# Hybrid decoder trunk on one core: nine groups of eight TensorE transposes become 144 VectorE block transposes

## The reference, cut to what matters

```python
for l in range(DEPTH):                       # 2
    h = _rmsnorm(x, ln_g[l])
    u = h @ w_in[l]                          # 2048 x 6232
    (g_a, g_b, g_c, g_d, a_q, a_k, a_v, a_lr, b_xbc, b_dt,
     c_q, c_kv, c_kr, d_q, d_k, d_v) = _split(u, IN_WIDTHS)
    y_a = _gla(a_q, a_k, a_v, log_a, ...) * silu(g_a)          # gated linear attention
    y_b = _ssd_mixer(b_xbc, b_dt, g_b, ...)                    # state-space mixer
    q   = _rmsnorm(c_q) @ w_uq;  kv = _rmsnorm(c_kv) @ w_ukv   # latent attention (MLA)
    y_c = _mla(...) * silu(g_c)
    y_d = _dilated_attention(dq, dk, d_v) * silu(g_d)
    x = x + concatenate([y_a, y_b, y_c, y_d]) @ w_out[l]       # 2048 x 2048
```

## Time and profile before

| | before |
|---|---|
| time, median of 3 runs (lowest to highest) | 830.31 us (829.94 to 830.39) |
| time of the profiled execution | 830.58 us |
| its span, first to last instruction | 828.5 us |
| PE busy | 823.1 us, 99% |
| DVE busy | 564.2 us, 68% |
| ACT busy | 481.7 us, 58% |
| granted TensorE clock, mean | 1.000 |

### The profile page before, as it was taken

One profiled execution on the slowest core, in us unless ns is written; L12 is line 12 of the kernel. 1 busy time (PEld: TensorE's weight loads), 2 busy tenths in 40 slices (PEclk: granted clock), 3 DMA queues, 4 the chain that ended last, 5 costly groups with the idle time before them and its releaser, 6 DMA issues.

```text
span 828.5 us, 11412 instructions
## 1 busy us (share of the span) xinstructions
PE 823.1 (99%) x4316; PEld 701.5 (85%) x4316; DVE 564.2 (68%) x974; ACT 481.7 (58%) x796; POOL 54.7 (7%) x63
## 2 busy tenths in 40 slices
PE   8999999999999999999999999999999999999998
PEld 6888888999888888888888888889998888888886
DVE  6665773877886986644664667639769868965542
ACT  6675544877865566443446465447787565654341
POOL 7100000120200000000000000003002000000000
PEclk9999999999999999999999999999999999999999
DMA  9974653476654346656666656526766443456553
GB/s 331 340 249 160 192 183 97 127 232 177 205 178 152 127 131 200 198 186 198 187 200 192 194 148 195 177 82 163 209 188 213 157 151 128 141 189 206 200 186 118
DMA packets 47606, 150.98 MB, mean 182 GB/s; under 512 B 5504, under 2 KB 6192, under 8 KB 47552
## 3 DMA queue, kind: packets, MB, share of 16 engines
q1 hardware_dynamic: 47040, 149.98, 57.2%
q10 hardware_dynamic: 320, 0.21, 0.1%
q0 software_dynamic: 192, 0.07, 0.0%
HBM read 148.13 MB, written 2.11 MB: 181 GB/s over the span
## 4 chain that ended last, share of the span: by engine, by line
PE 99%; DMA 0%; ACT 0%; DVE 0%; SPq 0%; DVEq 0%; issue 0%
PE gemm L661 29%; PE gemm L662 28%; PE gemm L670 28%; PE pairs L738 2%; PE pairs L873 1%; PE pairs L862 1%; PE pairs L854 1%; PE pairs L849 1%; PE pairs L850 1%; PE pairs L811 1%; PE pairs L888 1%; DMA raw<-in_weights_dram 0%; PE pairs L900 0%; PE pairs L901 0%; PE pairs L899 0%; PE pairs L603 0%
## 5 line engine op out<-in xcount | busy, mean ns | idle before, releaser
L1384 DVE TENSOR_TENSOR w_lo<-raw,w_hi 128x1024 fp32r<-128x1024 f32 (+2 forms) x295 | 325.5, 1111 | 201.9 <-ACT w_hi L1012 200.2
L661 PE MATMUL gemm<-w_hi,a_hi 128*128 128x512 f32 (+1 forms) x1144 | 422.3, 375 | 0.0
L662 PE MATMUL gemm<-w_hi,a_lo 128*128 128x512 f32 (+1 forms) x1144 | 414.4, 368 | 0.0
L1012 ACT ACTIVATE w_hi<-raw 128x1024 fp32r<-128x1024 f32 (+2 forms) x295 | 281.1, 967 | 182.9 <-PE gemm L670 155.1
L670 PE MATMUL gemm<-w_lo,a_hi 128*128 128x512 f32 (+1 forms) x1144 | 281.1, 368 | 0.0
L661 PEld LDWEIGHTS gemm<-w_hi,a_hi 128*128 128x128 f32 x1144 | 215.2, 188 | 34.8 <-issue 1.3
L662 PEld LDWEIGHTS gemm<-w_hi,a_lo 128*128 128x128 f32 x1144 | 215.3, 188 | 32.8
L670 PEld LDWEIGHTS gemm<-w_lo,a_hi 128*128 128x128 f32 x1144 | 203.6, 188 | 35.0
L566 POOL TENSOR_TENSOR st<-st,powers 128x4 f32<-128x4 f32 (+2 forms) x8 | 11.8, 1481 | 441.9 <-ACT arena L1096 218.3
L1221 ACT ACTIVATE arena<-arena,st 128x128 f32<-128x128 f32 (+1 forms) x32 | 13.1, 444 | 35.3 <-DVE st L1630 35.3
L1042 ACT ACTIVATE u<-gemm,st 128x512 f32<-128x512 f32 (+1 forms) x40 | 22.1, 605 | 17.6 <-PE gemm L670 17.6
(11 more groups left out here) (203 smaller groups left out, 618.0 us busy)
## 6 DMA issues: line engine op xcount, KB each, us to landing
raw<-in_weights_dram SPq DMA_DIRECT2D x225, 512.0 KB, 3.7
raw<-in_weights_dram SPq DMA_DIRECT2D x64, 278.0 KB, 3.0
raw<-in_weights_dram SPq DMA_DIRECT2D x6, 384.0 KB, 3.5
x<-in_x_dram SPq DMA_DIRECT2D x4, 512.0 KB, 6.2
o<-ssd_rows SPq DMA_DIRECT2D x8, 256.0 KB, 4.8
param_rows<-in_params_dram SPq DMA_DIRECT2D x2, 904.0 KB, 7.9
u<-in_xT_dram SPq DMA_DIRECT2D x3, 512.0 KB, 8.5
out_dram<-x SPq DMA_DIRECT2D x3, 512.0 KB, 5.5
```

Source lines behind the costliest of these rows:

```text
L661: pe.matmul(acc_t[t], a_hi[:, k, tok[t]], hi, start=k == 0, stop=False)
L662: pe.matmul(acc_t[t], a_lo[:, k, tok[t]], hi, start=False, stop=False)
L1012: A_(w_hi[:, g % SPLIT, 0:c], raw[:, g % RAW, 0:c], ACT.Copy).then_inc(hi_done, 1)
L1384: TT(w_lo[:, g % SPLIT, 0:c], raw[:, g % RAW, 0:c], w_hi[:, g % SPLIT, 0:c].bitcast(F32), ALU.subtract).then_inc(split_done, 1)
```

## The change

Nine groups of eight PE transposes leave: `gla_qk`, `mla_cT` and `ssd_yb` in each layer, and `xT` for blocks 0, 1 and 2. In their place DVE makes 16 block transposes each, of 32 partitions by 256 elements, from SBUF to SBUF. The copies of ACT at L1057, L1058 and L1168 leave with them; the scale 1/8 goes into the exponential of `gla_E` as a bias. `cT_hi` and `cT_lo` are now made from the turned rows in SBUF, and `ssd_add` writes its sum to a place of its own.

```diff
-PE_AT = {"gla qk": 16, "gla lr": 19, "gla z": 21}
+PE_AT = {"gla lr": 19, "gla z": 21}
...
-          "ssd xs": 62, "mla cT": 64, "mla q 0": Q_AT, ... "ssd Y": 76, "ssd yb": 81, "mla qT": 85, ...
+          "ssd xs": 62, "mla q 0": Q_AT, ... "ssd Y": 76, "mla qT": 85, ...
...
+Y_ROWS = [79, 80, 84, 85]
-X_NEXT = {UNITS - 6: 0, UNITS - 4: 1}
+X_NEXT = {UNITS - 21: 0, UNITS - 13: 1, UNITS - 5: 2}
...
+        xturned = [u[:, 0, j * 1024:(j + 1) * 1024].rearrange("p (k s) -> p k s", k=4) for j in range(3)]
+        ysum = A(6656, 1024)
+        cturned = A(3072, 1024, "p (k s) -> p k s", k=4)
...
@@ PE @@
-                    if l and n in (0, 2):
-                        xT(2 + n // 2, l)
+                    if l and n == 2:
+                        xT(3, l)
-                    if l + 1 < DEPTH and n in X_NEXT:
-                        xT(X_NEXT[n], l + 1)
@@ ACT @@
-                    A_(v[:, :, B:2 * B], v[:, :, B:2 * B], ACT.Exp, scale=1.0 / GLA_TAU)...
+                    A_(v[:, :, B:2 * B], v[:, :, B:2 * B], ACT.Exp, bias=log_scale, scale=1.0 / GLA_TAU)...
-                    act_.wait_ge(*pe("mla cT"))
-                    act_.wait_ge(*me("mla crs sum"))
-                    A_(cT_hi[:, :, :], pair_of("mla cT").rearrange(...), ACT.Copy)...
+                    act_.wait_ge(*dve("mla turn"))
+                    A_(cT_hi[:, :, :], cturned, ACT.Copy)...
@@ DVE @@
+                def gla_turn(i):
+                    v.wait_ge(*act("evac 0"))
+                    last = turn(o[:, 2].rearrange(...), u[:, :, 0:WB], (i,))
+                def ssd_rows(f):
+                    v.wait_ge(*me("ssd yT"))
+                    to = o[:, GB].rearrange("p t (k f b) -> p t k f b", f=4, b=32)
+                    part = ysum.rearrange("p (k t i a) -> p t k i a", k=4, t=T, i=4)
+                    for i in range(4):
+                        last = v.transpose(to[32 * i:32 * i + 32, :, :, f, :], part[32 * f:32 * f + 32, :, :, i, :])
+                def mla_turn(i):
+                    v.wait_ge(*me("mla cn"))
+                    last = turn(cturned, u[:, :, COL["cq"]:COL["cq"] + WB], (i,))
...
-                    if n == 17:
+                    if 14 < n < 19:
+                        gla_turn(n - 15)
+                    if n == 19:
                         gla_dots()
-                    if n == 18:
+                    if n == 20:
                         gla_diagonal()
-                        if n == 19 + i:        # memsets
+                        if n == 21 + i:
...
+                    if 62 <= n < 66:
+                        mla_turn(n - 62)
...
+                    if n in Y_ROWS:
+                        ssd_rows(Y_ROWS.index(n))
...
+                    if l + 1 < DEPTH and n in X_NEXT:
+                        j = X_NEXT[n]
+                        v.wait_ge(x_updated, updated(l, j))
+                        turn(xturned[j], x[:, :, j * WB:(j + 1) * WB]).then_inc(*sig(f"x turn {j}"))
```

More of the change, by code:

```diff
@@ L231 @@
     "act":
-        "x rs sum, evac 0, evac 1, gla q, gla k, gla lr, gla abs, gla exp, gla ln, evac 2, gla E 0, gla E 1, "
+        "x rs sum, evac 0, evac 1, gla lr, gla abs, gla exp, gla ln, evac 2, gla E 0, gla E 1, "
         "gla E 2, gla cross, gla E 3, gla E 4, evac 3, gla E 5, gla E 6, gla E 7, evac 4, ssd xT 0, ssd abs, ssd exp, "
@@ L693, in yT @@
                     last.then_inc(*signal("pe", f"yT {j}"))
[L695 to L705, removed]
                 def gla_lr():
                     pe.wait_ge(*act("evac 1"))
+                    pe.wait_ge(consts_in, 16 * 2)
                     ps = bank()
@@ L812, in ssd_Y @@
                     last.then_inc(*signal("pe", "ssd Y"))
[L814 to L831, removed]
                 token_banks = [None, None]
@@ L913, in mla_rT @@
                     heads_T("mla rT", lambda t, h: rr[:, t, h])
-                run = {"gla qk": gla_qk, "gla lr": gla_lr, "gla z": gla_z,
-                       "gla out": gla_out, "ssd xs": ssd_xs, "ssd cum": ssd_cum, "ssd gcol": ssd_gcol, "ssd CB": ssd_CB, "ssd Y": ssd_Y, "ssd yb": ssd_yb, "mla cT": mla_cT,
+                run = {"gla lr": gla_lr, "gla z": gla_z,
+                       "gla out": gla_out, "ssd xs": ssd_xs, "ssd cum": ssd_cum, "ssd gcol": ssd_gcol, "ssd CB": ssd_CB, "ssd Y": ssd_Y,
                        "mla qT": mla_qT, "mla kT": mla_kT, "mla rT": mla_rT}
@@ L1051, in evac @@
                         act_.preload_act_table_set("natural_log_exp_and_others")
[L1053 to L1058, removed]
                 def gla_lr():
@@ L1080, in gla_E @@
                     A_(v[:, :, 0:B], v[:, :, 0:B], ACT.Exp, scale=-1.0 / GLA_TAU)
-                    A_(v[:, :, B:2 * B], v[:, :, B:2 * B], ACT.Exp, scale=1.0 / GLA_TAU).then_inc(*signal("act", f"gla E {n}"))
+                    A_(v[:, :, B:2 * B], v[:, :, B:2 * B], ACT.Exp, bias=log_scale, scale=1.0 / GLA_TAU).then_inc(*signal("act", f"gla E {n}"))
                 def gla_cross():
@@ L1178, in mla_cT @@
                 def mla_cT():
-                    act_.wait_ge(*pe("mla cT"))
-                    act_.wait_ge(*me("mla crs sum"))
-                    A_(cT_hi[:, :, :], pair_of("mla cT").rearrange("p b (k s) -> p (b k) s", k=2), ACT.Copy).then_inc(*signal("act", "mla cT"))
+                    act_.wait_ge(*dve("mla turn"))
+                    A_(cT_hi[:, :, :], cturned, ACT.Copy).then_inc(*signal("act", "mla cT"))
                 def mla_q(t):
@@ L1465, in _ @@
                 acc8 = acc.rearrange("p r t a q -> p (r t a) q")
+                def gla_turn(i):
+                    v.wait_ge(*act("evac 0"))
+                    last = turn(o[:, 2].rearrange("p t c -> p (t c)").rearrange("p (k s) -> p k s", k=4), u[:, :, 0:WB], (i,))
+                    if i == 3:
+                        last.then_inc(*sig("gla turn"))
                 def gla_dots():
@@ L1564, in ssd_add @@
                     v.wait_ge(*act("ssd xD"))
-                    TT(bsq, bsq, pair_of("ssd Y"), ALU.add).then_inc(*sig("ssd yT"))
+                    TT(two(ysum, 2), bsq, pair_of("ssd Y"), ALU.add).then_inc(*sig("ssd yT"))
+                def ssd_rows(f):
[4 more added lines that the diff above has]
+                        last = v.transpose(to[32 * i:32 * i + 32, :, :, f, :], part[32 * f:32 * f + 32, :, :, i, :])
+                    if f == 3:
+                        last.then_inc(*sig("ssd y"))
                 def ssd_norm():
```

53 lines of the change are left out of this document (26 added, 27 removed), and 1 row of the table ORDER.

## The result

| | before | after |
|---|---|---|
| time, median of 5 runs each, in turns (lowest to highest) | 829.94 us (829.78 to 830.39) | 834.13 us (833.95 to 835.67) |
| ratio to before, 95% interval | | 1.0050 (1.0036 to 1.0064) |
| profiled execution, its span | | 834.01 us, 832.1 us |
| granted TensorE clock, mean | 1.000 | 0.996 |

A forecast was written before the change was run, and what follows sets the result against it. PE, busy for 99% of the span, was taken to bound the kernel. -8.0 + 2 x 4.3 + 2 x 1.0 = +2.6 us gave 833.2 us on the profiled execution, 832.9 against the median; 8-in-10 range 828 to 836.5.

The forecast's parts named there:

- What leaves PE, -8.0 us: On PE, seven groups of eight transposes at 0.90 us and two at 0.86 leave, 8.0 us, all on the chain.
- Price of a block transpose, 0.45 us: On DVE, each block transpose takes 0.45 us; the 144 new ones come to 65 us.
- Gated attention and x blocks, nothing: At n = 15 to 18 and n = 123, 131, 139, the los stay ahead of PE, so the transposes cost nothing.
- MLA's rows, 4.3 us per layer: At n = 62 to 65, turns delay lo(65) and the exp before hi(66) and hi(68); PE loses 4.3 us per layer.
- the last 1.3 of it for hi(68): At n = 68, PE waits for hi(68), late in ACT's queue: the last 1.3 us of the 4.3 per layer.
- n = 85, 1.0 us per layer: At n = 85, three fours of state-space rows ahead of lo(85) make PE wait 1.0 us per layer.
- No wait elsewhere: Outside MLA's rows and n = 85, no new PE waits; none at n = 16 to 20 and 123 to 143.
- The sum: Whole run: -8.0 + 2 x 4.3 + 2 x 1.0 = +2.6 us on the profiled 830.58; 832.9 against the median, chance 0.60.
- the buffers hide it all: Rival, whole loop: leads cover the transposes, faster at 822.6, or up to 828 with part of the waits; chance 0.18.
- Even: Rival: only the wait behind the exp is real, n = 85 is covered; +0.6 us, 830.9; chance 0.12.
- Lateness travels on: Rival, n = 71 to 77 and behind n = 85: another 1.5 us per layer, 836; chance 0.10 together with the clock.
- The clock falls: Rival, PE in the new waits: half speed adds 1.55 us per narrow unit; chance 0.10 together with lateness.

The follow-up runs named there:

- the kernel with the rows late: Changed kernel with three of the four state-space row parts moved from n = 80, 84, 85 to n = 85, 86, 87, behind lo(85); 835.49 us.
- the kernel with more load: Changed kernel with 16 block transposes more at n = 119 of both layers, whose result nothing reads; 835.48 us.
- heads first: Changed kernel with the decay exponents of two heads each at n = 62 and 63 instead of one each at 62 to 65; 832.59 us.

## Why the prediction was right, point by point

- **What leaves PE, -8.0 us:** right, 0.89 to 0.91 us for each group among the wide units in every kernel that is without it. MLA's, put back, cost 0.88 (2.43 for the unit instead of 1.55), where 0.86 was forecast.
- **Price of a block transpose, 0.45 us:** right for all three sources (1.78 us for four, 7.18 for sixteen). The Trainium skill, page "VectorE: DVE Perf Modes", section "The three transpose paths", gives 311 ns on VectorE and 390 ns on TensorE for a 128x128 transpose in bf16; in float32 the runs have 7.2 us for eight on VectorE against 0.89 us on TensorE, so the measurement decides. The same page's rule that such a transpose belongs on TensorE holds for MLA's rows (putting them back wins 7.4 us) and fails for gated attention and x (leaving them on VectorE wins 3.9 us against before). The state-space rows are nearly even, 0.4 to 0.6 us better on TensorE, which the intervals do not tell from nothing.
- **Gated attention and x blocks, nothing:** right. lo(17) is 1.5 us early, lo(124) 1.7 us, lo(141) 3.4 us, and with only these parts the loop has no wait. The tightest is lo(19), 0.8 us early as forecast, and only 0.1 in the profile with MLA's rows back on PE, where unit 14 was late: it is free by little.
- **MLA's rows, 4.3 us per layer:** the size was right (4.36, 4.49), and so were the places and sizes of the first two waits, 1.0 and 2.0 us. The step that failed is "the last 1.3 of it for hi(68)": PE's clock fell during or soon after the wait for hi(66), units 66 and 67 together took 1.3 to 1.5 us longer, and this used the time in which PE would have waited for hi(68). Layer 0 with the state-space rows on PE, where the clock stayed up, has the 1.31 as forecast. That the size still came out has a reason, as hi(68) would have held PE for those 1.3 us anyway, and some luck: a stretch twice as long, in one layer of the kernel with the rows late, cost 1.4 us on top. I had priced the lower clock as an addition, among the rivals; where another queue sets the next start, it is not one.
- **n = 85, 1.0 us per layer:** right in layer 1 and in both layers of the kernel with MLA's rows on PE (0.96 to 0.98), too small in layer 0 of the profiled execution (1.65). The difference comes from the weights of n = 70, a term that the forecast did not have: hi(70) waits for them, as ACT has nothing left ahead of it there, and what they are late goes on through the two queues to lo(85). Counted from hi(68), hi(70) ends 6.7 us later in layer 0 of the changed kernel and lo(85) 47.6; in the kernel with more load, both layers, it is 6.2 and 47.2, and unit 85 loses 0.97 and 1.06; in layer 0 of heads first it is 7.1 and 48.1, and n = 81 to 85 lose 2.0. Below 6.2 another step sets the time (5.7 and 47.1 in layer 1 of the changed kernel). What made the same load take 3.3 us once and 4.4 another time is open.
- **No wait elsewhere:** wrong by 0.2 us per layer at n = 103. This wait is gone in both kernels without the state-space rows on DVE, so it is theirs, 18 units later.
- **The sum:** +2.6 forecast on the profiled execution, +3.9 by units: 0.25 from n = 65 to 68, 0.63 from n = 85, 0.4 from n = 103. So the places were foreseen better than the total: the loss against before came out at 4.2 us where 2.6 was forecast.
- **Rivals:** "the buffers hide it all" falls with the waits seen; it is true for five of the nine groups. "Even" falls with n = 85. "Lateness travels on" is the 0.2 at n = 103 and no more. "The clock falls" happened; its price was nearly nothing in most places (at most 0.2 us over the 4.34 without it), and 1.4 us once.

The version to keep is the one with gated attention and x blocks on DVE and the rest on PE: 826.29 us, 3.9 us below the kernel before and 7.8 below the changed one. With the state-space rows on DVE as well (826.71) it can't be told apart by the intervals, but that kernel has waits and this one has none in its loop.

## What to carry to other kernels

An engine at 75% busy can be the one that holds up the engine at 99%: read for each moved instruction what stands behind it in its in-order queue, and how early that is over its user, at the place where the user's period is shortest. Move work to a spare engine only where this lead is longer than the piece, count pieces that follow each other before the lead has grown back, and follow the queue to the second engine that waits for it (here an exp with three weight roundings behind it). Look also for a weight load whose landing sets that queue: late by half a microsecond, it showed in full at the first unit without a lead, 15 units later. Moving such a piece later mostly moves the wait.

## What the runs showed of the hardware

The granted clock stood at its upper level for the whole loop before. In layer 0 of the changed kernel PE had worked for 0.78 of 2.0 us, between waits of 0.77 and 1.75 us, when it fell to the lower one for 3.4 us. Four profiled kernels have these two waits in both layers, eight cases. In six it was low for 3.4 us, in one for 6.8 us, beginning between 0.8 us before the end of the second wait and 1.5 us after it. In the eighth, layer 0 of the kernel with the state-space rows on PE, the clock stayed up. So such a fall can't be counted on or excluded from the waits alone; I have no row that tells the cases apart. With waits of at most 0.77 us close together (heads first, n = 64 to 68) it stayed up, and also at the single wait of 1.23 us at n = 85. The Trainium skill, page "TensorE: Matmul & The Clock Gate", Part 1, says that a monitor of PE's activity switches its clock between full and half rate; the trace agrees with both levels (matmuls of 278 columns every 0.13 and every 0.23 us).

A weight load of n = 70 (278 KB) took between 2.8 and 4.5 us from issue to landing, by profile and layer, though it stood at the same place of the queue each time.
